# Hybrid mLSTM and gated linear attention block: a chunk's output is copied by ACT, and half of the first mixer's gatings stand one slab later

## What is computed

```python
h = rmsnorm(x, mix_norm_g);  u = h @ w_in             # columns: mq mk mv mo mi mf | gq gk gv gr ga
h_m = mlstm_chunkwise(silu(conv(mq)), silu(conv(mk)), mv, log_i, log_f)    # first mixer, 4 heads of 128
h_m = head_rmsnorm(h_m, mlstm_norm_g) * sigmoid(mo)                        # its gating
h_g = gla_chunkwise(gq, gk, gv, log_a)                # second mixer: gated linear attention
h_g = head_rmsnorm(h_g, gla_norm_g) * silu(gr)
x = x + concat(h_m, h_g) @ w_out
x = x + softmax(rmsnorm(x) @ wq_x @ k.T / 16) @ v @ wo_x
x = x + square(relu(rmsnorm(x) @ w1)) @ w2
return rmsnorm(x, final_norm_g)
```

```python
A = einsum(qc, kc, exp(b_t - b_s));  o = A @ vc + (qc * exp(b)) @ S
S = exp(bL) * S + (kc * exp(bL - b)).T @ vc
```

## Time and profile before

| | us |
|---|---|
| median of three runs | 2824.75 |
| lowest and highest run | 2824.34, 2829.38 |
| profiled execution, whole | 2822.39 |
| its span in the profile | 2820.9 |
| PE busy in the span | 2795.1 (99%) |
| DVE busy | 1826.1 (65%) |
| ACT busy | 1512.7 (54%) |
| POOL busy | 1052.9 (37%) |
| share of PE in the chain that ended last | 97% |

### The profile page before, as it was taken

One profiled execution on the slowest core, in us unless ns is written; L12 is line 12 of the kernel. 1 busy time (PEld: TensorE's weight loads), 2 busy tenths in 40 slices (PEclk: granted clock), 3 DMA queues, 4 the chain that ended last, 5 costly groups with the idle time before them and its releaser, 6 DMA issues.

```text
span 2820.9 us, 44868 instructions
## 1 busy us (share of the span) xinstructions
PE 2795.1 (99%) x15012; PEld 2327.5 (83%) x15012; DVE 1826.1 (65%) x3043; ACT 1512.7 (54%) x3126; POOL 1052.9 (37%) x1334
## 2 busy tenths in 40 slices
PE   8999999999999999999999999999999999999998
PEld 8888788888878788888888878888888878888887
DVE  6376765776686755556688675466668675545665
ACT  6554444566655444555565544456656544455553
POOL 5264554665354400234546320044435550023440
PEclk9999999999999999999999999999999999999999
DMA  6732576565552222355654222255556222334442
GB/s 217 250 105 68 166 269 244 184 213 150 149 188 83 76 84 91 111 172 156 167 180 136 68 83 90 90 157 179 144 149 201 82 69 90 90 104 143 149 150 82
DMA packets 185906, 393.41 MB, mean 139 GB/s; under 512 B 14224, under 2 KB 14368, under 8 KB 185664
## 3 DMA queue, kind: packets, MB, share of 16 engines
q1 hardware_dynamic: 160112, 309.89, 36.0%
q0 software_dynamic: 22880, 75.72, 8.0%
q10 hardware_dynamic: 2672, 4.76, 0.5%
HBM read 346.24 MB, written 33.59 MB: 135 GB/s over the span
## 4 chain that ended last, share of the span: by engine, by line
PE 97%; DVE 2%; issue 1%; ACT 1%; DMA 0%; DVEq 0%; ACTq 0%
PE bank L1975 43%; PE work L1975 22%; PE bank L2338 17%; PE work L2338 3%; PE work L1989 1%; PE bank L2376 1%; PE bank L1989 1%; PE work L2037 1%; PE work L2091 1%; PE bank L2059 1%; PE work L2236 1%; PE work L2240 1%; PE work L2219 1%; PE work L2235 1%; DVE qk L1598 0%
## 5 line engine op out<-in xcount | busy, mean ns | idle before, releaser
L897 ACT ACTIVATE w_hi<-raw 128x512 fp32r<-128x512 f32 x1156 | 724.8, 630 | 1006.4 <-PE bank L1975 509.9
L1411 DVE TENSOR_TENSOR w_lo<-raw,w_hi 128x512 fp32r<-128x512 f32 x657 | 483.9, 740 | 790.8 <-ACT w_hi L897 789.2
L1409 DVE SCALAR_TENSOR_TENSOR w_lo<-raw,w_hi 128x512 fp32r<-128x512 f32 x499 | 448.2, 919 | 95.3 <-ACT w_hi L897 94.8
L729 POOL TENSOR_TENSOR hr<-qk 128x256 f32<-128x256 f32 x60 | 44.9, 749 | 781.4 <-ACT qk L1285 781.4
L2338 PE MATMUL bank<-w_hi,h_hi 128*128 128x512 f32 x720 | 280.2, 389 | 0.1
L2338 PE MATMUL bank<-w_hi,h_lo 128*128 128x512 f32 x720 | 280.1, 389 | 0.0
L2338 PE MATMUL bank<-w_lo,h_hi 128*128 128x512 f32 x720 | 280.1, 389 | 0.0
L1975 PE MATMUL bank<-w_hi,x_hi 128*128 128x512 f32 x640 | 256.6, 401 | 0.0
L1975 PE MATMUL bank<-w_lo,x_hi 128*128 128x512 f32 x640 | 250.6, 392 | 0.0
L1975 PE MATMUL bank<-w_hi,x_lo 128*128 128x512 f32 x640 | 250.3, 391 | 0.0
L719 POOL TENSOR_TENSOR h_lo<-qk,h_hi 128x256 fp32r<-128x256 f32 x180 | 184.2, 1044 | 73.3 <-ACT h_hi L1298 73.3
(11 more groups left out here) (403 smaller groups left out, 6464.8 us busy)
## 6 DMA issues: line engine op xcount, KB each, us to landing
raw<-in_w_dram SPq DMA_DIRECT2D x226, 512.0 KB, 3.9
raw<-sums_dram SPq DMA_DIRECT2D x120, 512.0 KB, 3.8
raw<-in_w_in_dram SPq DMA_DIRECT2D x112, 512.0 KB, 3.6
raw<-in_w_out_dram SPq DMA_DIRECT2D x32, 512.0 KB, 3.8
raw<-kq_dram SPq DMA_DIRECT2D x32, 512.0 KB, 3.8
raw<-vo_dram SPq DMA_DIRECT2D x32, 512.0 KB, 3.7
xres<-in_x_dram POOLq DMA_DIRECT2D x16, 512.0 KB, 6.2
early_rows<-in_w_dram POOLq DMA_DIRECT2D x8, 1024.0 KB, 8.2
```

The lines of the kernel that those rows point to most:

```text
L729: nc.gpsimd.tensor_tensor(diff[:, kt, :], quarter(0, 0, kt), quarter(0, 1, kt), ALU.subtract).then_inc(diff_ready, 1)
L897: nc.scalar.activation(w_hi[:, slot, :], raw[:, pair_slot, slot % 2, :], ACT.Copy).then_inc(slab_hi, 1)
L1409: ins = stt(out=w_lo[:, slot, :], in0=src, scalar=1.0, in1=hi, op0=ALU.mult, op1=ALU.subtract)
L1411: ins = tt(w_lo[:, slot, :], src, hi, ALU.subtract)
```

## The change

Two things are moved. ACT makes the copy of a chunk's output, in front of its squares, and waits for `o_full` instead of `o_out`; DVE has neither the copy nor the wait any more. And of the sixteen gatings of the first mixer in DVE's slab 49, those of heads 2 and 3 stand in slab 50, behind the two level sums of that slab.

```diff
@@ ACT, slot 0 of a chunk @@
-                        act.wait_ge(o_out, 4 * g + c)
+                        act.wait_ge(o_full, 4 * g + c)
+                        nc.scalar.activation(tok[:, c - 1, COLS:], work[:, 2, :], ACT.Copy).then_inc(o_out, 1)
                         for h in range(HEADS):
@@ DVE, slot 0 of a chunk @@
                         ins.then_inc(s_ready, 1)
-                        dve.wait_ge(o_full, 4 * g + c)
-                        nc.vector.tensor_copy(tok[:, c - 1, COLS:], work[:, 2, :]).then_inc(o_out, 1)
@@ DVE, slabs 49 and 50 @@
                     if s == 49:
                         read_out(dve, g, 4 * B_MO + 3)
                         dve.wait_ge(num_out, 4 * g + 4)
-                        gate_heads(0, HEADS)
+                        gate_heads(0, HEADS, (0, 1))
+                    if s == 50:
+                        gate_heads(0, HEADS, (2, 3))
```

## The result

The change made the kernel slower. The median of ten runs is 2833.78 us (2830.92 to 2837.41) against 2826.39 (2821.49 to 2830.74) for the kernel before: 7.4 us more, a ratio of 1.0027 with a 95% interval of 1.0017 to 1.0036. The profiled execution has a span of 2829.4 us in place of 2820.9.

A forecast was written before the change was run, and what follows sets the result against it. PE bounds the kernel, busy 99% of the span; its stop before slab 51 was to come back before slab 56. +0.1 (chain) + 4.8 (clock) = +4.9 us on 2824.75 gave 2829.7 us, range 2823.5 to 2834.

The forecast's parts named there:

- the landing of the last move: POOL's moves ahead of slab 56: the last issue lands 2.1 us later, at 314.45 in the first group.
- against before: Chain from DVE's gatings through POOL to PE at slab 56, against the kernel before: +0.1 us over four groups.
- the clock: Dips of PE's granted clock after the new stops before slab 56: 1.2 us a group, 4.8 us in all.
- The old stop goes: PE before the level products: second mask ends at 298.88, 0.7 us before slab 50 is done, so no stop.
- The gatings and the moves: First group: last gating ends at 301.93, 5.0 us later than before; POOL begins its moves at 302.64.
- at 314.45: First group: the last move lands then instead of at 309.4, and DVE, there at 310.1, waits some 4.3 us.
- I take 1.2: Clock cost per group after the stop before slab 56, below 1.3 since part of a dip can fall into the stop.
- the whole dip: Upper bound for the low clock after a stop of PE, 1.75 us, as in the first group before.
- +6.9: Sum if all four dips last 3.4 us at 0.50 wholly on work: 6.8 us of clock in place of 4.8.
- The faster one: Rival: DVE need not wait for the moves, PE runs through slab 56; 13.5 us less, 2811.3 us, chance 0.08.
- The slower rival: Rival: weight loads hold the moves up by 1 us a group; +11, 2836 us, chance 0.12.
- the rival with the whole dip in every group: Rival: each group pays 1.75 us of low clock at slab 56; +7.1, 2831.9 us, chance 0.28.

The follow-up runs named there:

- copy_only: The change without its second part: ACT copies the output, all sixteen gatings stay in slab 49; 2812.51 us against 2822.35 for the kernel before, ratio 0.996.
- gatings_only: The kernel before with the gatings split over slabs 49 and 50, DVE's copy kept; 2836.36 us against 2822.35, ratio 1.0048.
- early_gatings: The kernel before with the copy on ACT, gatings of chunks 0 and 1 in slab 47, the rest in slab 49; 2808.51 us against 2822.35, ratio 0.9946.
- early_dve_copy: The kernel before with gatings of chunks 0 and 1 in slab 47, the rest in slab 49, DVE's copy kept; 2810.74 us against 2824.53, ratio 0.9947.
- all_behind: The change, but with all sixteen gatings behind the level sums of slab 50; 2843.49 us against 2824.53 for the kernel before, ratio 1.0064.
- act_moves: The change, but with eight of the sixteen moves issued from ACT's queue in slab 51; 2814.52 us against 2822.35 for the kernel before, ratio 0.9971.

## Why the prediction was wrong

The forecast was no change, 2829.7 us and +4.9; it came to +7.4, which is clear of no change. The measured time lies inside the range, by 0.2 us. Of the 4.1 us between 2829.7 and 2833.78, 1.6 are not the change's at all: the kernel before has a median of 2826.39 over ten runs, where the forecast started from 2824.75. The mechanism was the one foreseen, step by step. What failed were two terms of the sum that were too small: the landing of the last move, taken as 2.1 us, which made "against before" +0.1 us where +1.5 was measured, and the clock, taken as 4.8 us where 5.6 was measured.

- **The old stop goes: right.** No wait is left at line 2092. The second mask ends at 298.13, 0.7 us before slab 50 does, in the first group. Left out of the sum was that the moved copy brings DVE's whole stretch forward by 0.6 us against PE: its gatings begin 4.57 us ahead of slab 50 in the change and 4.58 in copy_only, but 3.94 before and in gatings_only. It was lost again, since the first mask then waited 0.56 us for PE.
- **The gatings and the moves: right.** The last gating ends 5.33 us after the first matmul of slab 50, forecast 5.34 (301.93 - 296.59); POOL begins at 6.03, forecast 6.05.
- **The landing: mis-sized.** I took 2.1 us for the last move from the earlier trace rows; for the last three of the first group it was 2.5 to 2.8, and for the last one of each group 2.3 to 2.7. DVE's transposes began 18.24 us after slab 50 in the first group, where the step "at 314.45" gives 17.86. In the four groups they began 0.38, 0.18, 0.37 and 0.65 us later than that, 1.6 us together, which is about the difference between the +1.5 us of the table's first pair and the forecast of +0.1. The rows name what was missed: the earlier trace rows are moves that come 8 to 10 us behind a weight load, and with the moves 5 us later that load stands among them. No run moves the load alone; that it is the load rests on the order of the sixteen landings, which is the same in the four groups, and on copy_only, where a load beside the last move goes with a landing of 4.1 to 4.4 us in each group.
- **The clock: mis-sized.** "I take 1.2" a group gave 4.8; measured were 1.6, 1.6, 0 and 2.3, together 5.6. A dip came behind three of four stops, the rate that the earlier trace rows showed, but where it came it cost about what the whole dip costs (1.6 us for 1.75) or, in the fourth group, more. My reason for going below the whole dip, that part of it could fall into the stop, held only in the fourth group, where 1.7 us did, but where the clock was low for twice as long as well. In the first two groups the dip fell wholly on work. The sentence beside it with the rule of the Trainium skill (TensorE: Matmul & The Clock Gate, Terms) gave +6.9 and came nearer; its rule agrees with the rows in so far as 3.4 us at 0.50 cost 1.6.
- **Elsewhere: not in the sum.** 1.4 us between the profiles, no more than the same stretches differ between the kernels here. With it the terms make +0.1 + 1.4 + 5.6 + 1.4 = 8.5 us between the two profiled executions; between the medians it is 7.4.
- **The rivals.** The faster one, moves that are not late, would have been 13.5 us. The change is not that case, but the runs bear out the size, since early_gatings and early_dve_copy, which have neither stop, gained 13.8 us each. The rule beside it, of the Trainium skill (DMA: Bandwidth & Descriptors, SWDGE vs HWDGE vs iDMA), by which POOL could issue faster beside an idle DVE, is not borne out by the trace: POOL's sixteen issues took 10.37 us in the change and 10.34 before, and the last three, beside a DVE that waited, took 0.651 us each where they had taken 0.648. No run shows whether DVE's instructions here are of the modes that the page means. The slower rival, moves still later because weight loads hold them up, came true in part: it was 0.4 us a group where it was priced at 1. The time that came is that of the rival with the whole dip in every group (+7.1), though by another way: three groups with dips, one of them twice as long, and late landings. That it lies so near is luck.

What stays open: why the third group has no dip behind a stop of 3.5 us, and what makes a dip short or long. The part of the 1.4 us elsewhere that no row shows is open too. None of it was tried.

## What to carry to other kernels

Work that is moved out of the way of one wait has readers of its own: here the gatings fed a chain of some 12 us of moves on another queue, whose slack was 5.1 us and whose delay was 5.0 plus what the removed stop gave to PE. Compare the slack of that chain with the delay and with the gain together, since PE comes earlier once the stop is gone. Of two measures against the same stop, try each alone: the copy by itself gave 9.8 us, and moving half of the gatings turned this into a loss, while moving them forward into idle time gave 13.8.

## What the runs showed of the hardware that was not expected

- Eight moves issued from ACT's queue took 6.39 us of ACT, 0.8 us each (over all four groups 0.64 to 1.42, the median 0.66), no less than POOL's 0.65; the issues held ACT for all that time, and the split behind them came late.
- A move of 64 KB that took 2.1 us to land on a quiet stretch took 4.1 to 4.5 us right behind the issue of a 512 KB weight load (297.56 before, 305.48 in the change, 306.90 in copy_only), and the moves issued behind it, 0.65 us apart, needed some ten issues to come back to 2.1 us. For a chain that ends in a landing it matters at which of its transfers the load comes.
- The clock fell after long stops of PE and not after short ones, with no sharp edge between: the granted clock was at 0.50 behind all four stops of about 5.9 us (all_behind) and all four of 4.1 to 4.5 us (gatings_only), behind three of four of 3.3 to 4.1 us (the change), three of four of 1.9 to 2.0 us (before) and one of four of 1.0 to 1.7 us (act_moves), the longest; seven stops of up to 0.6 us (copy_only) had no dip behind them.
